# Gates kept and moved in pairs of first keys, the expert loop's first buffers moved elsewhere

## What is computed

```
s = einsum('thpk,hpnk->thpn', q, sub_keys)      # scores of first and second keys
top_s, pos = top_k(s1 + s2 sums, 16);  g = softmax(top_s)
a = gelu(einsum('tkd,td->tk', expert_u[ix], hx))
out = einsum('tk,tkd->td', gx * a, expert_v[ix])
```

## Time and profile before

| what | us |
|---|---|
| median of 3 runs | 1838.03 (1837.93 to 1838.91) |
| profiled execution, its own time | 1834.78 |
| its span | 1832.9 |
| TensorE busy in the span | 1668.9 (91%) |
| VectorE busy | 1512.3 (83%) |
| ScalarE busy | 643.2 (35%) |
| POOL busy | 936.8 (51%) |

### The profile page before, as it was taken

How to read it: one execution, slowest core, us unless ns; L and a number is a source line. 1 busy time by engine, 2 the same in 40 slices (tenths; PEclk the granted TensorE clock), 3 DMA queues, 4 the chain that set the end, 5 groups by cost and what they waited for, 6 DMA issues and landing times.

```text
span 1832.9 us, 28781 instructions
## 1 busy us (share of the span) xinstructions
PE 1668.9 (91%) x9338; PEld 1442.3 (79%) x9338; DVE 1512.3 (83%) x3069; ACT 643.2 (35%) x1085; POOL 936.8 (51%) x771
## 2 busy tenths in 40 slices
PE   4999998999945885799999999999999999999994
PEld 2776766479944875699999999999999999999993
DVE  0732275458999996799999999999999999999997
ACT  1222265122104783233333333333333333333331
POOL 1111000014403664578887887777666666666661
PEclk9999999999977998799999999999999999999997
DMA  9445102040000889999999999999999999999993
GB/s 354 168 176 212 54 1 104 35 184 2 1 24 1 190 191 282 348 402 406 400 404 392 405 401 398 407 407 406 404 406 403 402 401 397 398 398 407 408 398 135
DMA packets 256532, 518.22 MB, mean 283 GB/s; under 512 B 114004, under 2 KB 131028, under 8 KB 256342
## 3 DMA queue, kind: packets, MB, share of 16 engines
q1 hardware_dynamic: 180432, 244.94, 37.5%
q0 software_dynamic: 73728, 268.47, 37.0%
q10 hardware_dynamic: 2310, 4.04, 0.6%
HBM read 486.45 MB, written 30.93 MB: 282 GB/s over the span
## 4 chain that ended last, share of the span: by engine, by line
PE 51%; DVE 24%; issue 12%; DMA 7%; ACT 2%; DVEq 1%; SPq 1%; POOL 0%; POOLq 0%; ACTq 0%; PEldq 0%
DVE arena L1443 11%; PE ps L1756 10%; PE ps L1755 10%; PE ps L1754 10%; PE ps L1843 4%; PE ps L1728 4%; DMA U_in<-in_expert_uT 3%; DMA arena_w<-in_w_mod 2%; PE ps L1569 2%; PE ps L1570 2%; PE ps L1573 2%; DVE V_lo L1391 2%; PE ps L1667 1%; DMA arena_w<-in_w_in 1%; DVE C_lo L1420 1%
## 5 line engine op out<-in xcount | busy, mean ns | idle before, releaser
L1756 PE MATMUL ps<-hT_hi,U_lo 128*128 128x384 f32 x1024 | 343.7, 336 | 0.0
L1754 PE MATMUL ps<-hT_hi,U_hi 128*128 128x384 f32 x1024 | 343.5, 335 | 0.0
L1755 PE MATMUL ps<-hT_lo,U_hi 128*128 128x384 f32 x1024 | 343.0, 335 | 0.0
L1754 PE MATMUL ps<-V_hi,C_hi 128*128 128x512 f32 x768 | 301.5, 393 | 34.5 <-DVE C_lo L1420 34.5
L1756 PE MATMUL ps<-V_hi,C_lo 128*128 128x512 f32 x768 | 303.4, 395 | 0.0
L1755 PE MATMUL ps<-V_lo,C_hi 128*128 128x512 f32 x768 | 303.2, 395 | 0.0
L522 POOL DMA_INDIRECT arena<-in_expert_u,idxn x128 | 176.6, 1380 | 82.4 <-issue 31.8
L873 ACT CAST V_hi<-V_in 128x1024 fp32r<-128x1024 f32 x128 | 135.0, 1055 | 235.0 <-PE ps L1756 220.0
L522 POOL DMA_INDIRECT arena<-in_expert_v,idxn x128 | 159.0, 1242 | 93.1 <-DVE arena L1443 42.5
L910 ACT ACTIVATE act_t<-ps 128x384 f32<-128x384 f32 x128 | 62.9, 492 | 388.2 <-PE ps L1756 388.2
L1754 PEld LDWEIGHTS ps<-hT_hi,U_hi 128*128 128x128 f32 x1024 | 192.3, 188 | 4.9
(11 more groups left out here) (283 smaller groups left out, 3302.7 us busy)
## 6 DMA issues: line engine op xcount, KB each, us to landing
U_in<-in_expert_uT SPq DMA_DIRECT2D x128, 512.0 KB, 9.1
V_in<-in_expert_v SPq DMA_DIRECT2D x126, 512.0 KB, 6.3
arena_w<-in_w_mod SPq DMA_DIRECT2D x12, 2048.0 KB, 12.4
gate_in<-gates_scratch SPq DMA_DIRECT2D x126, 192.0 KB, 7.4
gates_scratch<-arena_w SPq DMA_DIRECT2D x5, 4096.0 KB, 20.9
arena_w<-in_w_in SPq DMA_DIRECT2D x4, 2048.0 KB, 8.6
arena_w<-in_w_query SPq DMA_DIRECT2D x4, 2048.0 KB, 11.1
arena_w<-in_w_out SPq DMA_DIRECT2D x2, 2048.0 KB, 8.4
```

Source lines behind the costliest of these rows:

```text
L1754: nc.tensor.matmul(out, hi, rhi, start=start, stop=False)
L1755: nc.tensor.matmul(out, hi, rlo, start=False, stop=False)
L1756: return nc.tensor.matmul(out, lo, rhi, start=False, stop=stop)
```

## The change

- The gate table in DRAM has one block per pair of first keys: `(64, 128, 6, 2, 64)`, so a half block of tokens is written in runs of 128 numbers (512 B), and a pair is loaded at once, 384 KB in runs of 3 KB, every second step. `gbuf` holds the two halves apart. VectorE reads the gates with a stride.
- `GCUT` is `(0, PAIRS)`: the last half block is one transfer, and ScalarE waits for all of it before it loads the gates of pairs 0 and 1.
- `V_in` lies elsewhere and is loaded early, together with U: blocks 0 and 1 before the gate stage, 2 during it. V of 0 is split within the gate stage, after quad 18 of the third block on ScalarE, and before the last six VectorE quads on VectorE. `V_hi`, `V_lo` lie in unused columns of `hT_hi`, `hT_lo`, and TensorE reads them as four pieces of 128 columns.
- Row buffers 0 to 5 lie where the first half of `gbuf` was (they wait for its third write), 6 and 7 where buffers 2 and 3 were.
- The loads of `XF` and `fing` move from ahead of SP's loop into it, after the loads for step 31.
- Loops are written over two pairs, four steps, in a turn.

```
-GCUT = (0, 24, 56, 88, 128)
+GCUT = (0, PAIRS)
+TWICE = PAIRS // 2
+HB = P // 2
...
-        gbuf = cutout(WO, NKEY * P).rearrange("p (i t) -> p i t", i=NKEY)
+        gbuf = cutout(WO, NKEY * P).rearrange("p (c i t) -> p c i t", c=2, t=HB)
...
+        V_hi, V_lo = [[t[:, :, lo:lo + P] for lo in (0, P + TD)] for t in (hT_hi, hT_lo)]
+        rowr = [rows_under[:, r, :] for r in range(6)] + [cutout(BO + 3072 + r * D, D) for r in range(2)]
...
-        gates_d = nc.dram_tensor("gates_scratch", (NB1, P, TD), f32, kind="Internal").ap()
+        gates_d = nc.dram_tensor("gates_scratch", (PAIRS, P, 2 * NDEN, 2, HB), f32, kind="Internal").ap()
...
             for j in range(2):
                 load_u(j, j)
+                load_v(j, j)
...
+                            sp.wait_ge(s_vlo, 1)
+                            load_v(2, 0)
                         continue
                     for r in range(len(GCUT) - 1):
-                        rows_ = slice(GCUT[r], GCUT[r + 1])
-                        sp.dma_start(to[:, rows_], gbuf[:, rows_, t0:t0 + P // 2]).then_inc(s_gpart[r], 16)
-            for n in range(2, 4):
-                sp.wait_ge(s_vlo, n - 1)
-                load_v(n, n % 2)
+                        pairs = slice(GCUT[r], GCUT[r + 1])
+                        sp.dma_start(to[:, pairs], held[:, pairs]).then_inc(s_gpart[r], 16)
+            sp.wait_ge(s_vlo, 2)
+            load_v(3, 1)
             for part in s_gpart:
                 sp.wait_ge(part, 16)
-            sp.wait_ge(s_c, 1)
-            load_gates(2, 0)
+
+            def load_pair(i, g):
                 for j in range(2):
                     n = i * 2 + j
                     sp.wait_ge(s_ulo, n - 1)
                     load_u(n, j)
                     sp.wait_ge(s_vlo, n - 1)
                     load_v(n, j)
-                    sp.wait_ge(s_c, n - 2)
-                    load_gates(n - 1, 1 - j)
+                    if j == 0:
+                        sp.wait_ge(s_c, n - 2)
+                        load_gates(i, g)
+            with sp.Fori(1, TWICE // 4) as i:
+                for g in range(2):
+                    load_pair(i * 2 + g, g)
             sp.wait_ge(s_spill, 16 * NBLK)
             for b in range(NBLK):
                 sp.dma_start(XF[:, b], x1_d[b * P:(b + 1) * P, :]).then_inc(s_xf, 16)
             sp.dma_start(fing, final_g.unsqueeze(0).broadcast_to([P, D])).then_inc(s_fing, 16)
+            with sp.Fori(TWICE // 4, TWICE) as i:
+                for g in range(2):
+                    load_pair(i * 2 + g, g)
...
-                if first and row == 2:
+                if first and row == 0:
+                    pool.wait_ge(s_gout[0], 16 * NDEN)
+                if first and row == 6:
                     pool.wait_ge(s_gq, QUADS * NDEN)
-                if first and row == 3:
+                if first and row == 7:
                     pool.wait_ge(s_gate, NBLK)
...
+                if b == NDEN and p == 18:
+                    split_v(0, 0, 1, True)
...
-                    if first and j == 0:
-                        act.wait_ge(s_gpart[2], 16)
...
             act.wait_ge(s_gpart[0], 16)
-            for j in range(2):
-                act.dma_start(V_in[:, j], expert_v[j * P:(j + 1) * P, :]).then_inc(s_vin[j], 16)
-                act.dma_start(gate_in[:, j], gates_d[j]).then_inc(s_gin[j], 16)
-            act.wait_ge(s_gpart[1], 16)
-            split_v(0, 0, 1, True)
+            for g in range(2):
+                act.dma_start(gate_in[:, g], gates_d[g].rearrange("p c e t -> p (c e t)")).then_inc(s_gin[g], 16)
...
             split_u(1, 1)
+            split_v(0, 0)
             gate_quads(3, 6)
```

More of the change, by code:

```diff
@@ L255, in program @@
         h2row = (H2[4], H2[0])
[L257 to L262, removed]
+        V_in = cutout(BO + 1024, 2 * D).rearrange("p (j d) -> p j d", j=2)
+        rows_under = sb("rows_under", [P, 6, D])
+        late = sb("late", [P, (NBLK + 1) * D])
+        between_ = sb("between_", [P, CO - WO - 12 * D])
         XF = late[:, 0:NBLK * D].rearrange("p (b d) -> p b d", b=NBLK)
@@ L266, in program @@
         hT_hi, hT_lo = sb("hT_hi", [P, KD, NBLK * P], f32r), sb("hT_lo", [P, KD, NBLK * P], f32r)
-        rows_mid = sb("rows_mid", [P, 2, D])
-        rowr = ([cutout(BO + 1024 + r * D, D) for r in range(4)] + [rows_mid[:, r, :] for r in range(2)]
-                + [rows_late[:, r, :] for r in range(2)])
+        gate_in = sb("gate_in", [P, 2, 2 * TD])
+        C_hi, C_lo = sb("C_hi", [P, 2, TD], f32r), sb("C_lo", [P, 2, TD], f32r)
+        act_t = sb("act_t", [P, 2, TD])
+        V_hi, V_lo = [[t[:, :, lo:lo + P] for lo in (0, P + TD)] for t in (hT_hi, hT_lo)]
+        rowr = [rows_under[:, r, :] for r in range(6)] + [cutout(BO + 3072 + r * D, D) for r in range(2)]
         tmp2 = [U_in[:, 0].rearrange("p k n -> p (k n)"), U_in[:, 1].rearrange("p k n -> p (k n)"), V_in[:, 0]]
@@ L408, in v_block, with gates_block @@
                 return expert_v[n * P:(n + 1) * P, :] if isinstance(n, int) else expert_v[ds(n * P, P), :]
-            def gates_block(n):
-                return gates_d[n] if isinstance(n, int) else gates_d[ds(n, 1)].rearrange("a p t -> (a p) t")
+            def gates_block(i):
+                block = gates_d[i] if isinstance(i, int) else gates_d[ds(i, 1)].rearrange("a p c e t -> (a p) c e t")
+                return block.rearrange("p c e t -> p (c e t)")
             def load_u(n, r):
@@ L457, in _ @@
                     load_v(n, j)
-                    sp.wait_ge(s_c, n - 2)
-                    load_gates(n - 1, 1 - j)
-            sp.wait_ge(s_c, NB1 - 2)
-            load_gates(NB1 - 1, 1)
+                    if j == 0:
[4 more added lines that the diff above has]
+                    load_pair(i * 2 + g, g)
+            sp.wait_ge(s_spill, 16 * NBLK)
+            for b in range(NBLK):
+                sp.dma_start(XF[:, b], x1_d[b * P:(b + 1) * P, :]).then_inc(s_xf, 16)
+            sp.dma_start(fing, final_g.unsqueeze(0).broadcast_to([P, D])).then_inc(s_fing, 16)
+            with sp.Fori(TWICE // 4, TWICE) as i:
+                for g in range(2):
+                    load_pair(i * 2 + g, g)
             for n, b in enumerate(FIN):
@@ L884, in _ @@
                 act.wait_ge(s_gq, q + 1)
-                act.copy(gbuf[:, :, p * QUAD:(p + 1) * QUAD],
+                at = p % HALFQ * QUAD
+                act.copy(gbuf[:, p // HALFQ, :, at:at + QUAD],
                          ps[:, 2 + q % 4, :].rearrange("p (t n) -> p n t", t=QUAD)).then_inc(s_gev, 1)
@@ L1404, in _, with experts @@
             split_u(1, 1)
+            split_v(0, 0)
             gate_quads(3, 6)
             choose(4, 0, 0, 0, (0, 0))
-            def experts(i, last, row):
+            def experts(turn, g, last, row):
+                i = turn * 2 + g
+                dve.wait_ge(s_gin[g], 16 * (turn + 1))
+                weights = gate_in[:, g].rearrange("p (c e t) -> p e c t", e=2, t=HB)
                 for j in range(2):
                     n = i * 2 + j
-                    dve.wait_ge(s_gin[j], 16 * (i + 1))
                     dve.wait_ge(s_ge, n + 1)
-                    dve.tensor_tensor(act_t[:, j], act_t[:, j], gate_in[:, j], ALU.mult).then_inc(s_c, 1)
+                    sums = act_t[:, j].rearrange("p (c t) -> p c t", t=HB)
+                    dve.tensor_tensor(sums, sums, weights[:, j], ALU.mult).then_inc(s_c, 1)
                     row(i, 4 * j)
@@ L1478, in norm3, with turns @@
                                          op0=ALU.mult, op1=ALU.mult).then_inc(s_y, 1)
[L1480 to L1485, removed]
+            def turns(lo, hi, row):
+                with dve.Fori(lo, hi) as turn:
+                    for g in range(2):
+                        experts(turn, g, False, row)
+            for g in range(2):
+                experts(0, g, False, dot_row(0))
+            turns(1, TWICE // 4, dot_row(0))
+            turns(TWICE // 4, TWICE // 2, dot_row(1))
             coefs(0)
             dve.wait_ge(s_acc0, 1)
-            with dve.Fori(PAIRS // 2, 3 * PAIRS // 4) as i:
-                experts(i, False, add_row(0))
+            turns(TWICE // 2, 3 * TWICE // 4, add_row(0))
             coefs(1)
-            with dve.Fori(3 * PAIRS // 4, PAIRS - 1) as i:
-                experts(i, False, add_row(1))
+            turns(3 * TWICE // 4, TWICE - 1, add_row(1))
+            experts(TWICE - 1, 0, False, add_row(1))
             residual(0)
-            experts(PAIRS - 1, True, add_row(1))
+            experts(TWICE - 1, 1, True, add_row(1))
             residual(1)
@@ L1878, in sums_v @@
                     for half in range(2):
-                        col = slice(half * NC, (half + 1) * NC)
+                        col = slice(half * 4, (half + 1) * 4)
                         last = products3(ps[:, 2 + 2 * b + half, :], C_hi[:, j, tok], C_lo[:, j, tok],
-                                         V_hi[:, j, col], V_lo[:, j, col], start, stop)
```

(8 more changed lines are left out.)

41 lines of the change are left out of this document (19 added, 22 removed).

## The result

The change made the kernel slower by 0.19%, at the edge of what the measurement can tell: 1841.16 us (median of 20 runs, 1837.10 to 1845.85) against 1837.63 (20 runs, 1834.11 to 1844.25), ratio 1.0019 with a 95% interval of 1.0010 to 1.0027. That is +3.5 us where +3.0 was forecast, and 0.16 us above the forecast median of 1841.0.

The account below looks back on a forecast made before the run. TensorE was taken to bound the loop at 8.31 us a step, VectorE and DMA nearly level. Terms 0 + 3.3 - 11.3 + 11 + 0 = +3.0 us on 1838.03 gave 1841.0 us, range 1831 to 1851 (8 in 10).

Parts of the forecast that it names:

- Where it could gain: TensorE's waits for C_lo before the first sums (23.15 us) and step 2 (9.18): gain only there while TensorE sets the step.
- The gate stage: V of 0's added VectorE subtraction (1.22 us) against ScalarE's vanishing waits (0.99 and 0.47): 0, within -1.5 to +1.2 us.
- The last write: Last half block of gates: 14.5 us in 512 B runs plus eight POOL rows beside it, landing after 24.8 us.
- the rival of full rate: Last gate write: 512 B runs go at full rate, 10.3 us, giving 1836.8 us in total; chance 0.15.
- From the write to the first sums: Gate loads, ScalarE's table and gelu, then 4.5 us from gates' multiply: first sums at 740.7, 3.3 us later (-2.2 to +10).
- The second wait: TensorE's 9.18 us wait at step 2 goes, with 2.15 us of slow start: -11.3 us.
- The same loads in the loop: Moved XF and fing loads make U of 32 12 to 13.3 us late; wait 8.3 to 9.6 plus slow start: +11 us.
- the cushion of 3.7: At step 2, U was 12.90 us late and TensorE stood 9.18, so 3.7 us of lateness cost no wait.
- Pairs of gates and strides: In the loop, paired gate loads and strided places for V cost nothing: 0 us.
- Loads hidden in the loop: U of 32 comes in time behind the moved loads: 1835 us with half the wait gone, 1830 with all; chance 0.20.
- Odd U late: In the loop, odd U blocks come late in every pair, 0.15 to 0.3 us each: 1850 to 1859 us; chance 0.17.
- slower reads of V: TensorE reads V's pieces slower over 2304 matmuls; 4 ns each give 1850 us; chance 0.05.

Follow-up runs that it names:

- v_late: Changed kernel with V of 0 split on VectorE behind its last six quads instead of ahead of them; one run, 1840.02 us.
- rows_held: Changed kernel with POOL holding rows 2 to 7 until the last gate write has landed; 1833.36 us, ratio 0.9978 to the kernel before.
- The second execution: The changed kernel without any edit, executed again on another chip; 1841.81 us, ratio 1.0037 to the kernel before.
- xf_spread: Changed kernel with the six late loads (XF and fing) issued one at a time, 16 steps apart, in the loop; 1828.33 us, ratio 0.9948 to the kernel before.
- before_xf_in_loop: Kernel before with only the XF and fing loads moved into the loop, after the loads for step 31; 1840.45 us, ratio 1.0016.
- three: Changed kernel with late loads spread, the last gate write's first 8 pairs as their own transfer, rows 4 to 7 held until the rest landed; 1818.48 us.

## Why the prediction was right

It was right in the sum and in nearly every mechanism. Two of its terms were too small, by some 0.7 and by 2.3 to 2.9 us, and one was too large by 1. That the median came out 0.16 us from the forecast is partly luck, since these errors add up to 2.0 to 2.6 us by the profiles.

**Where it could gain.** Right: only the two waits of TensorE moved; the step stayed 8.31 us with TensorE busy throughout.

**The gate stage**, 0 forecast within -1.5 to +1.2: about +0.7 (404.6 and 404.8 to the last write without the change, 405.2 to 406.2 in the ten executions with it). The forecast's parts are in the trace: ScalarE's two waits of the earlier trace rows are gone, and TensorE waits 3.10 us for VectorE's quads where it waited 2.04. That V alone is the cause isn't shown, since `v_late` brought the 2.04 back and saved nothing; POOL was the next to be late. The two traces fit a subtraction that costs its 1 us at either place, once through TensorE's wait and once through POOL; a run without it was not made.

**The last write**, 24.8 us forecast with the rows: 25.3. Its share in the price of a run is shown by the five half blocks ahead of it. View of their line, first after the change, where each run is 512 B:

```profile
DMA to landing us min/median/max: 16.1/16.2/16.9
```

and before, at 256 B:

```profile
DMA to landing us min/median/max: 20.8/20.9/21.3
```

The difference is 4.7 us and the estimate from three sizes said 19.1 - 14.5 = 4.6. A window in which such a write runs shows the same (columns as in the earlier trace rows, to be read beside the 219 GB/s of the earlier trace rows):

```profile
601.00:615.00 14.00, 13.12 (x113) 11.50 (x111) 12.20 (x46) 11.84 (x24) 9.52 (x12) 1.00 0.94 269
```

269 GB/s over 16 engines is 30.5 ns for a run of 512 B, 28.6 of them busy; 28.4 were estimated. Of the rival of full rate (10.3 us) nothing is left: it asked for 8.8 us less. The Trainium skill ("DMA: Bandwidth & Descriptors", Specifications), by whose smallest size for line rate that rival stood, doesn't fit this kernel's rows; at 512 B a run still costs more than its bytes. The share of six of the eight rows is shown by `rows_held`.

**From the write to the first sums**: 9.0 us forecast, 7.9 measured, since the gates landed 3.3 us after their issue, not 4.0, and ScalarE's issue of both took less. The last piece, gates' multiply to first sums, was 4.50 as in the earlier trace rows. Start: +2.3 for a forecast of +3.3. The clock times named as signs, 731 to 733 for the write's landing and 740 to 742 for the first sums, were passed by 3 and 2 us (736.2, 744.08), because all that lies ahead of the write's issue took 4.3 us longer in this execution (710.89 for 706.60); counted from the issue they hold to 1 us.

**The second wait**, -11.3: right. The two gelu intervals around it were 15.70 and 12.23 us before, 11.3 over two steps; after the change both are plain steps.

**The same loads in the loop**, +11: the mechanism was right in place, cause and size of the transfer, and the term was 2.3 to 2.9 us too small. U landed 24.5 us after the issue of V of 31, where 22.5 to 23.8 was worked out, and ScalarE wanted it at 9.5, where 10.5 was; so 15.06 us late where 12 to 13.3 was said, and with the cushion of 3.7 the wait is 11.33, as measured. The gelu intervals are 17.86 and 12.62 us, 13.9 over two steps. The second execution lies nearer the forecast, with U 13.93 us late, a wait of 10.20 and 13.2 us over the same two steps. That the six loads are the cause is shown by `xf_spread` (wait gone, 12.4 us less) and `before_xf_in_loop` (wait there with the move alone). 24.5 us at 409 GB/s are 10.0 MB, while only 4.2 MB and a remainder stood in SP's queue up to the end of U: more than half went to what the other queues and later issues had. That is what the Trainium skill says of turns between queues ("DMA: Bandwidth & Descriptors", Queues, rings and completion order), and the trace agrees as far as this sum goes.

**Pairs of gates and strides**, 0: right. A step is 8.306 us before and after; the V matmuls take 394 ns in the mean and took 393, the subtraction for V 1216 and took 1221.

**The sum.** By the stretches of the table the change is +0.5, +2.3 and +2.0 to +2.6, that is +4.8 to +5.5 us, against one profile of the kernel before; by the runs it is +3.5 (1.8 to 5.0) and, on another chip, +6.1 (4.4 to 9.2). The forecast of +3.0 was a little low, for the loop's wait. Split by the stretches, the move alone gives +2.7 and all the rest +0.1 and +3.0 in its two executions, so the parts add up within that spread. By the runs they don't quite: +3.9 for the move and +3.8 or +2.1 for the rest are more than +3.5.

**The rivals.** Loads hidden in the loop: out as written, since the wait is there; but what it hoped for is to be had when they are spread. Full rate at 512 B: out. Odd U late and slower reads of V: out, by the step's time of 8.306 us.

**Open.** Why the wait at step 2 is 6.75 and 7.40 us with the new layout and 9.18 with the old was not tried alone; nor was what sets the length of the slow stretch of TensorE's clock near 240 us, and whether that goes with the kernel or with the execution.

## What to carry to other kernels

A block of loads that nobody needs soon must not stand in one piece ahead of a load with no slack, neither ahead of a saturated loop nor in it: moving it only moves the wait (9.18 to 11.33 us), while one load every 16 steps made it free (-12.4 us). When a big write gates the next stage, look at what else is allowed onto the DMA engines meanwhile, since each of those bytes is paid at full price (-7.3 us for six held rows). Writing first the part that is needed first pays in full only when nothing with no slack is queued behind the rest: alone it gave 4.2 us, and with the late loads spread and four rows held it belongs to the fastest kernel here, 18 us under the one before.

## What the runs showed of the hardware that was not expected

- A DMA issue isn't free when a large write is unfinished: SP stood 7.47 us at one issue of 512 KB that takes 0.33 in the loop, and 1.15 in `three`, where four of POOL's rows were held back. What exactly the issue waits for was not tried.
- POOL is slower beside VectorE's subtractions of 1024 columns: four one-hot rows took 6.43 us beside three of them (694.48 to 697.97), 5.38 beside two and 4.32 beside one (both in `v_late`), 3.30 beside none.
- At 512 B a run still costs: 4 MB landed in 16.2 us, and in 20.9 at 256 B.
